# VectorE's second operand kept in PSUM: taps in a bank of their own, gates, residuals and rotations written back

## The reference

```
u = x*(1+sc1) + sh1                     # sc, sh, g from silu(c) @ w_ada
z = u @ w_in + b_in                     # 78 tiles of 128 columns
A: mLSTM       h = num / max(|den|, exp(-m));  y_a = sigmoid(o) * norm(h)
B: attention with a latent cache (prompt: causal; samples: 1024 past rows in 8 pages)
C: convolution y[t] = b + sum_k w[k]*full[t+k], k = 0..30; silu(norm(y))
D: retention   with q, k rotated: x1*cos - x2*sin, x1*sin + x2*cos
out = (sum_n sigmoid(gates_n) * (y_n @ w_branch_n)) @ w_out
x = norm(ALPHA*x + g1*out)
x = norm(ALPHA*x + g2*ffn(x))           # SwiGLU
```

## Time and profile before

| | us |
|---|---|
| three runs | 1928.85, 1932.64, 1932.87; median 1932.64 |
| profiled execution | 1932.92 |
| its span, first to last instruction | 1931.2 |
| PE, weight loads, DVE, ACT, POOL busy | 1733.7, 1490.1, 933.2, 740.0, 694.8 |
| mean granted PE clock | 0.941 of the upper level |

### The profile page before, as it was taken

The page is one execution under the profiler, slowest core; times in us unless marked ns, Lnnn a source line. Parts: engine busy times, 40 slices in busy tenths (PEclk is TensorE's granted clock), DMA queues, the critical chain, the costliest instruction groups (busy, mean ns, idle before and its releaser), DMA issues. The chain is left out here.

```text
span 1931.2 us, 30401 instructions
## 1 busy us (share of the span) xinstructions
PE 1733.7 (90%) x10994; PEld 1490.1 (77%) x10994; DVE 933.2 (48%) x1937; ACT 740.0 (38%) x1122; POOL 694.8 (36%) x418
## 2 busy tenths in 40 slices
PE   3899899998799979999839998999987999799997
PEld 1788789886377759999718987888853788599996
DVE  1454577468631563333323535774785315633333
ACT  1456434333334244443224564342233341544422
POOL 0434546545023313332113445455540233133321
PEclk8899999999899989999969999999997999899999
DMA  9242365246754354444072432652666643544440
GB/s 357 88 177 93 98 105 183 102 154 229 304 205 165 133 199 155 150 152 153 23 282 88 183 110 76 106 195 88 205 234 254 240 169 109 207 146 150 153 151 30
DMA packets 81184, 309.12 MB, mean 160 GB/s; under 512 B 23746, under 2 KB 33282, under 8 KB 50946
## 3 DMA queue, kind: packets, MB, share of 16 engines
q1 hardware_dynamic: 81026, 307.09, 46.3%
HBM read 291.81 MB, written 15.25 MB: 159 GB/s over the span
## 5 line engine op out<-in xcount | busy, mean ns | idle before, releaser
L1980 POOL TENSOR_TENSOR wlx<-ring,wh 128x1024 fp32r<-128x1024 f32 x172 | 410.7, 2388 | 754.8 <-ACT wh L1030 749.9
L430 PE MATMUL zps<-uhi,wh 128*128 128x320 f32 x1232 | 387.3, 326 | 0.0
L431 PE MATMUL zps<-ulo,wh 128*128 128x320 f32 x1232 | 374.1, 315 | 0.0
L1030 ACT ACTIVATE wh<-ring 128x1024 fp32r<-128x1024 f32 x172 | 182.3, 1060 | 394.8 <-PE zps L431 262.8
L2072 POOL TENSOR_TENSOR wlo<-ring,whi 128x1024 fp32r<-128x1024 f32 x66 | 161.9, 2452 | 367.2 <-ACT whi L1030 367.2
L430 PEld LDWEIGHTS zps<-uhi,wh 128*128 128x128 f32 x1232 | 240.3, 195 | 12.8 <-issue 8.4
L431 PEld LDWEIGHTS zps<-ulo,wh 128*128 128x128 f32 x1232 | 240.6, 195 | 0.8
L889 PE MATMUL zps<-xhi,whi 128*128 128x320 f32 x704 | 220.1, 313 | 2.3 <-DVE xlo L1942 2.0
L891 PE MATMUL zps<-xhi,wlo 128*128 128x320 f32 x704 | 219.1, 311 | 0.0
L890 PE MATMUL zps<-xlo,whi 128*128 128x320 f32 x704 | 219.1, 311 | 0.0
L435 PE MATMUL zps<-uhi,wlx 128*128 128x320 f32 x1248 | 211.4, 312 | 0.0
(11 more groups left out here) (268 smaller groups left out, 2573.6 us busy)
## 6 DMA issues: line engine op xcount, KB each, us to landing
ring<-wpack_dram SPq DMA_DIRECT2D x222, 1024.0 KB, 4.9
arena<-cache_dram SPq DMA_DIRECT2D x128, 320.0 KB, 4.6
arena<-stateA_dram SPq DMA_DIRECT2D x2, 2064.0 KB, 9.8
o_cn_s<-arena SPq DMA_DIRECT2D x2, 2064.0 KB, 11.1
arena<-stateD_dram SPq DMA_DIRECT2D x2, 2048.0 KB, 11.8
o_ret_s<-arena SPq DMA_DIRECT2D x2, 2048.0 KB, 11.5
x<-o_y SPq DMA_DIRECT2D x2, 1280.0 KB, 7.5
o_y<-x SPq DMA_DIRECT2D x4, 640.0 KB, 3.0
```

The source lines that it names most:

```text
L430: nc.tensor.matmul(o, hi[:, k * P:(k + 1) * P], xh[:, k, :], start=k == 0, stop=False)
L431: last = nc.tensor.matmul(o, hi[:, k * P:(k + 1) * P], xl[:, k, :], start=False, stop=False)
L1030: return nc.scalar.activation(out, in_, func, **kw).then_inc(*ev(sem, label))
L1980: G().tensor_tensor(wlx[:, n % RING, half], ring[:, n % RING, half], wh[:, i, :], ALU.subtract).then_inc(*ev("pool_l", (q, i)))
```

## The change

Four `mps` banks are left to PE, and the fifth, `taps_ps`, is DVE's alone for the taps: two tiles of 256 columns fill it. The partial sums stay there; the last tap of a tile writes to `y`, and the tiles 2 and 3 wait for the last tap of 0 and 1. In `rotate` the sin halves come first and the cos product is written over the tile's own `zps` bank, which is then released by the sum. In `gated` the product of the first branch goes straight to `gsum`, with no copy; the others write the product over the bank and add it from there. In the residual the gated product is written over the bank, which is released by the sum (`"r"`) in place of the product (`"g"`). The denominators read `num` from PSUM twice, as max(-den, floor) and then max(den, that), with two instructions where there were three (copy, absolute value, maximum). What is computed stays the same.

```diff
--- before.py
+++ after.py
@@ -340,7 +340,8 @@
         cnp = vm[:].rearrange("p h t -> p (h t)")[:, 0:H * W].rearrange("p (h d) -> p h d", h=H)
 
         zps = [ctx.enter_context(nc.psum_tensor(f"zps{i}", [P, 512], F32)) for i in range(3)]
-        mps = [ctx.enter_context(nc.psum_tensor(f"mps{i}", [P, 512], F32)) for i in range(5)]
+        mps = [ctx.enter_context(nc.psum_tensor(f"mps{i}", [P, 512], F32)) for i in range(4)]
+        taps_ps = ctx.enter_context(nc.psum_tensor("taps_ps", [P, 512], F32))
         banks = {}
 
         FIRST_FFN = BLOCKS.index(("ffn", 0))
@@ -385,7 +386,7 @@
                 @block.tensor
                 def _(pe):
                     zi, mi, bi, turned = [0], [0], [0], [0]
-                    zfree, mfree = [None] * 3, [None] * 5
+                    zfree, mfree = [None] * 3, [None] * 4
 
                     def bank(kind, name, freed_by):
 
@@ -678,7 +679,7 @@
                     conv_tiles(3, lambda: row_scores(2), lambda: outputs("a", 0, W))
 
                     def turned_tile(x_, j, *fill):
-                        in_tiles((f"{x_}{j}", f"{x_}{j + 1}"), [("dve_dk", ("t3", x_, h)) for h in (j, j + 1)], fill=fill)
+                        in_tiles((f"{x_}{j}", f"{x_}{j + 1}"), [("dve_dk", (x_, h)) for h in (j, j + 1)], fill=fill)
 
                     def plain_tile(x_, j, *fill):
                         in_tiles((f"{x_}{j}", f"{x_}{j + 1}"), [("act_d", (x_, h)) for h in (j, j + 1)], fill=fill)
@@ -869,7 +870,7 @@
                         q = SPLIT.index(("out", i))
                         for j in range(2):
                             d = 2 * i + j
-                            split_tile(q, n, j, ("wo", d), ("dve_r", ("g", 1, d)), ghi, glo, ("act_go", "dve_gl") if d == 0 else None)
+                            split_tile(q, n, j, ("wo", d), ("dve_r", ("r", 1, d)), ghi, glo, ("act_go", "dve_gl") if d == 0 else None)
                             if d >= 2:
                                 mean_part(1, d - 2)
                         block_end[n] = ("pe_z", ("wo", 2 * i + 1))
@@ -904,7 +905,7 @@
                             last.then_inc(*ev("pe_z", name))
                     pe.wait_ge(*at("dve_f", FT - 1))
                     for d in range(KC):
-                        ps = bank("z", ("fo", d), ("dve_r", ("g", 2, d)))
+                        ps = bank("z", ("fo", d), ("dve_r", ("r", 2, d)))
                         for j in range(FT):
                             i = d * FT + j
                             if i % 16 == 0:
@@ -1643,11 +1644,10 @@
                             out = hh[0:tn, t, 2 * hp:2 * hp + 2, :]
                             if X == "a":
                                 den, rec = stats[0:tn, 80:82], stats[0:tn, 82:84]
-                                V().tensor_copy(rec, num[:, :, P]).then_inc(*ev(s, ("dc", t, hp)))
-                                dve.wait_ge(*at(s, ("dc", t, hp)))
-                                V().scalar_tensor_tensor(out=den, in0=rec, scalar=-1.0, in1=rec, op0=ALU.mult, op1=ALU.max).then_inc(*ev(s, ("abs", t, hp)))
-                                dve.wait_ge(*at(s, ("abs", t, hp)))
-                                V().tensor_tensor(den, den, col4[0:tn, t, 64 + 2 * hp:66 + 2 * hp], ALU.max).then_inc(*ev(s, ("den", t, hp)))
+                                floor = col4[0:tn, t, 64 + 2 * hp:66 + 2 * hp]
+                                V().scalar_tensor_tensor(out=rec, in0=num[:, :, P], scalar=-1.0, in1=floor, op0=ALU.mult, op1=ALU.max).then_inc(*ev(s, ("neg", t, hp)))
+                                dve.wait_ge(*at(s, ("neg", t, hp)))
+                                V().tensor_tensor(den, num[:, :, P], rec, ALU.max).then_inc(*ev(s, ("den", t, hp)))
                                 dve.wait_ge(*at(s, ("den", t, hp)))
                                 V().reciprocal(rec, den).then_inc(*ev(s, ("rec", t, hp)))
                                 dve.wait_ge(*at(s, ("rec", t, hp)))
@@ -1720,12 +1720,12 @@
                         if h == 0:
                             dve.wait_ge(*at("pe_m", ("a", "st", 3)))
                         ps, bias = z(f"{x_}{h}"), sw(f"{x_}{h}")
-                        V().scalar_tensor_tensor(out=dst, in0=ps[:, 0:T], scalar=bias, in1=cs("cosD"), op0=ALU.add, op1=ALU.mult).then_inc(*ev("dve_dk", ("t1", x_, h)))
                         for i, (to, of) in enumerate((((0, 64), (64, 128)), ((64, 128), (0, 64)))):
                             V().scalar_tensor_tensor(out=std[to[0]:to[1], :], in0=ps[of[0]:of[1], 0:T], scalar=bias[of[0]:of[1]], in1=cs("sinD")[of[0]:of[1]],
-                                                   op0=ALU.add, op1=ALU.mult).then_inc(*ev("dve_dk", (f"t{2 + i}", x_, h)))
+                                                   op0=ALU.add, op1=ALU.mult).then_inc(*ev("dve_dk", (f"t{1 + i}", x_, h)))
+                        V().scalar_tensor_tensor(out=ps[:, 0:T], in0=ps[:, 0:T], scalar=bias, in1=cs("cosD"), op0=ALU.add, op1=ALU.mult).then_inc(*ev("dve_dk", ("t3", x_, h)))
                         dve.wait_ge(*at("dve_dk", ("t3", x_, h)))
-                        V().tensor_tensor(dst, dst, std[:], ALU.add).then_inc(*ev("dve_dk", (x_, h)))
+                        V().tensor_tensor(dst, ps[:, 0:T], std[:], ALU.add).then_inc(*ev("dve_dk", (x_, h)))
 
 
                     dve.wait_ge(C.sem("in_hist"), 16)
@@ -1737,13 +1737,16 @@
                         for i in range(first, last):
                             j, k = 2 * (i // (2 * CW)) + i % 2, i % (2 * CW) // 2
                             wk = smallw[:, SM["cw"] + j * CW + k:SM["cw"] + j * CW + k + 1]
-                            o, src = y[:, 2, j, 0:SEQ], ucp[:, j, k:k + SEQ]
+                            part_sum, src = taps_ps[:, j % 2 * SEQ:(j % 2 + 1) * SEQ], ucp[:, j, k:k + SEQ]
+                            o = part_sum if k < CW - 1 else y[:, 2, j, 0:SEQ]
                             if k == 0:
                                 dve.wait_ge(*at("dve_c", ("glu1", j)))
+                                if j >= 2:
+                                    dve.wait_ge(*at("dve_c", ("tap", j - 2, CW - 1)))
                                 nc.vector.tensor_scalar(o, src, wk, sw("cb", j), ALU.mult, ALU.add).then_inc(*ev("dve_c", ("tap", j, k)))
                             else:
                                 dve.wait_ge(*at("dve_c", ("tap", j, k - 1)))
-                                nc.vector.scalar_tensor_tensor(out=o, in0=src, scalar=wk, in1=o, op0=ALU.mult, op1=ALU.add).then_inc(*ev("dve_c", ("tap", j, k)))
+                                nc.vector.scalar_tensor_tensor(out=o, in0=src, scalar=wk, in1=part_sum, op0=ALU.mult, op1=ALU.add).then_inc(*ev("dve_c", ("tap", j, k)))
 
                     rotate("dk", 0)
                     rotate("dk", 1)
@@ -1769,13 +1772,11 @@
                             dve.wait_ge(*at("act_gt", (n, d)))
                             ps = z(("br", n, d))
                             if n == GATE_ORDER[0]:
-                                V().tensor_tensor(gt[:, k, :], ps[:, 0:T], gt[:, k, :], ALU.mult).then_inc(*ev("dve_br", ("first", d)))
-                                dve.wait_ge(*at("dve_br", ("first", d)))
-                                V().tensor_copy(gsum[:, d, :], gt[:, k, :]).then_inc(*ev("dve_br", (n, d)))
+                                V().tensor_tensor(gsum[:, d, :], ps[:, 0:T], gt[:, k, :], ALU.mult).then_inc(*ev("dve_br", (n, d)))
                             else:
-                                V().tensor_tensor(g, ps[:, 0:T], g, ALU.mult).then_inc(*ev("dve_br", ("t", n, d)))
+                                V().tensor_tensor(ps[:, 0:T], ps[:, 0:T], g, ALU.mult).then_inc(*ev("dve_br", ("t", n, d)))
                                 dve.wait_ge(*at("dve_br", ("t", n, d)))
-                                V().tensor_tensor(gsum[:, d, :], gsum[:, d, :], g, ALU.add).then_inc(*ev("dve_br", (n, d)))
+                                V().tensor_tensor(gsum[:, d, :], ps[:, 0:T], gsum[:, d, :], ALU.add).then_inc(*ev("dve_br", (n, d)))
 
                     for t in range(3):
                         tokens("d", t)
@@ -1899,12 +1900,12 @@
                                         split(q)
                             ps = z((name, d))
                             dve.wait_ge(*at("dve_mod", 11 if which == 1 else 23))
-                            nc.vector.tensor_scalar_mul(tmp[:, d % 2, 0:SEQ], ps[:, 0:SEQ], mod[:, g + d, 0:1]).then_inc(*ev("dve_r", ("gp", which, d)))
-                            nc.vector.tensor_tensor(tmp[:, d % 2, SAMP].rearrange("p (b t) -> p b t", b=NB), ps[:, SAMP].rearrange("p (b t) -> p b t", b=NB),
+                            nc.vector.tensor_scalar_mul(ps[:, 0:SEQ], ps[:, 0:SEQ], mod[:, g + d, 0:1]).then_inc(*ev("dve_r", ("gp", which, d)))
+                            nc.vector.tensor_tensor(ps[:, SAMP].rearrange("p (b t) -> p b t", b=NB), ps[:, SAMP].rearrange("p (b t) -> p b t", b=NB),
```

(2 more changed lines are left out.)

## The result

The changed kernel takes **1916.3 us** (median of 11 runs) beside 1932.64 for the kernel before; the ratio is 0.9917, 95% interval 0.9901 to 0.9932. One of the 11 took 3379.28 us, for a reason that nothing here shows, and is left out of the ratio; the other ten lie between 1910.85 and 1923.88. That is 16.3 us less, by the ratio 16.0. Forecast were 1921.5 and 11.3 less, with 1913 to 1938 as the range. The profiled execution took 1919.91 us around a span of 1918.3.

The account below looks back on a forecast made before the run. PE, busy 90% of the span, was taken to bound the kernel. A layer gains 5.45+1.1+2.9-0.5-3.3 = 5.65 us, two layers 11.3; 1932.9-11.3 = 1921.6, given as 1921.5, with 8 in 10 from 1913 to 1938.

Parts of the forecast that it names:

- Denominators: Ahead of the scores behind `weigh`: PE starts 3.25 us sooner and the clock stays up, 2.2; 5.45 us a layer gained.
- Rival A: Behind the denominators the clock stays low, as 2 us of idle remain; without 2.2 us a layer, 1926; chance 0.20.
- Rotations: DVE's rotation sums lose their stalls, but PE's waits name none of them: 0 gained.
- Taps: DVE's five batches of taps, pitch 0.42 us with the sum in PSUM: 4.0 us a layer gained, 0.5 lost.
- rivals B and E: B: PSUM writes slow the taps, 1951 at pitch 0.67, chance 0.14. E: scalars in SBUF still stall, 1939, chance 0.02.
- First batch: Taps end some 9 us sooner, so the token copies no longer hold the first scores: 1.1 us a layer gained.
- Second batch: Taps behind which no PE wait ends: 0 gained.
- Fourth batch: 26 taps take 10.9 us in place of 17.2, so PE's L757 no longer waits: 2.9 us a layer gained.
- Third batch: PE's L757 waits for the copy behind these taps, so each slower tap is PE's loss: 0.5 us a layer.
- Four banks: PE's matmuls wait for bank releases in heads (1.75), last state group (0.9), three more places (0.65): 3.3 us a layer lost.
- Rival C: Four banks cost more than their sum: twice it, 1928, or 1937 if the clock also falls; chance 0.14.
- Rival D: The gain ends on a weight block's transfer, bound by the queue; the denominators' 5.45 would go: 1932; chance 0.10.

Follow-up runs that it names:

- e_den: The kernel before with only the denominators' two instructions, five matmul banks; 1911.78 us, ratio 0.9908.
- e_after: The changed kernel measured and profiled again, the same program; 1915.25 us, ratio 0.9914 to the kernel before.
- e_taps: The kernel before with four matmul banks and the taps accumulated in the fifth; 1930.57 us, ratio 1.0007.
- e_four: The kernel before with four matmul banks in place of five, the fifth unused; 1947.68 us, ratio 1.0088.
- e_rot: The kernel before with only the rotations summed from PSUM, five matmul banks; 1923.41 us, ratio 0.9968.
- e_notaps: The changed kernel with the taps back in SBUF and five matmul banks; 1907.35 us, ratio 0.9881 to the kernel before.

## Why the prediction came out right, and which steps did not

*Total.* The mechanism was right: an operand in PSUM ends the stalls, and only where PE waits for DVE does it pay. -11.3 was forecast and -16.3 measured. But four terms were far too small, three gains (10.9 forecast and 18.7 measured, 0 and 7.1, 7.0 and 17.1) and one loss (6.6 and 17.2), and what they missed cancelled in large part. That the sum came out within 5 us is luck as much as reckoning.

- *Denominators, 5.45 a layer forecast, 9.35 measured alone.* The place itself agrees: -6.0 in e_den against 3.25 for the idle plus 2.2 for the clock, plus 0.8 since five banks let the scores wait only 1.20. (The "idle of 5.5" counts the gate row's product as over after 0.5 us; the row has 4.97.) In the whole change it gave 2.3 and 3.6 in the two layers, 3.8 and 3.6 in e_after: the gate row waits 1.92 and the clock falls after all. Rival A was true there in half. The failed step is the one behind the denominators, what stands late next: I priced the wait of L641 for L1696 only as something that four banks would lengthen by 0.9. It went instead, 5.5 a layer in e_den, since DVE's last scaling escaped a GpSimd operation. In the whole change two waits of 0.9 and 0.5 are left there, and it gave 2.0 and 3.7 in one profile, 1.2 twice in the other.
- *Rotations, "0. [...] PE's waits name none of them".* Measured alone 3.5 a layer. The wait names L1696, which stands behind head norm and rotations in DVE's order; a line that no wait names was on the path of one that is named. Gates and residuals: 0 forecast, +2.4 measured with an interval that reaches no change.
- *Taps, 3.5 a layer forecast net, 8.6 measured* (e_taps against e_four). The pitch was right: 0.42 taken, 0.395 measured, and rivals B and E are out (no tap over 488 ns). First batch: 1.1 forecast; L1568 is gone from the waits. Second batch: "no PE wait ends on what stands behind it: 0" failed against e_four, where GpSimd, held by the taps, was what PE waited for: 2.7 a layer between the two columns. Fourth batch: 2.9 forecast, 5.2 to 5.8 seen when the values of sample 1 end, since L761's sixteen matmuls take 1.95 us at the upper clock. That the load of the next pages "moves with them" was right: PE waits for them 5.35 us before, 5.73 and 5.34 after; where some 4 us were lost again behind them, it was the clock. Third batch: 0.5 forecast as lost, 0.15 seen (L758 waits 1.04 in place of 0.89).
- *Four banks, 3.3 a layer forecast, 8.6 measured* (e_four). The places of the sum were wrong in part: the last state group lost 0.7 in waits (L642, 3.52 in place of 2.79) where 0.9 was forecast, and the heads 1.15 in waits where it was 1.75. Not in the sum stood the clock behind the gate row (1.9 there with the wait) and branch 3 (2.9 in the second layer, 2.3 in the first, GpSimd's wait above). The samples' 1.4 is within the spread of one profile. "From above, twice the sum" was too low, since the lower level behind the gate row lasted 10 us in place of 6.7. Rival C, taken alone, was true; it was paid for by the terms above.
- *Rival D is out.* PE's waits for weight blocks are 54.9 us in 14 before, 57.3 in 14 in the changed kernel and 55.3 in e_after: they did not grow by what the others lost.

What stays open. Alone, the parts add by their ratios to -19.9 us, the whole is -16.0 and -16.6 in two measurements; the intervals (about 6 us on the sum of four) don't tell these apart, so whether the parts disturb each other isn't shown. e_den's and e_rot's second-row gain is one and the same wait. e_notaps, with both, is clearly faster than e_rot, but not told apart from e_den (0.9881, 0.9855 to 0.9907, beside 0.9908, 0.9891 to 0.9925). Why one handover takes 0.46 and another 0.28 us for the same two instructions isn't shown either: it goes with the number of instructions ahead of it, and at retention's head norm it is 0.28 in every kernel. What decides whether the taps in SBUF or GpSimd's subtraction stands, and whether the lower level behind a page load lasts 6.8 or 13.7 us, is open, too.

## What to carry to other kernels

Before a DVE change is priced at nothing, walk back along DVE's order from every wait of PE for DVE, not only from the lines that the wait names: what stands ahead of it on the engine is on the path too. Where two engines meet at a fixed pitch (here a 2.4 us GpSimd subtraction every 4.8 us), ask how far each end is from a collision: 0.09 us more of lead was worth 5.5 us a layer, and no sum of durations shows it. Profile the same program twice before reading a stretch: here two profiles of one kernel differed by 9 us. And a PSUM bank given to one user for a whole layer can be lent while that user is idle: 11 to 14 us here for a few lines.

## What the runs showed of the hardware

- DVE writing PSUM costs about 8 ns for 256 columns (480 against 472 ns with the same operands), a chain through one bank none beyond that; reading the second operand from PSUM is no dearer than from SBUF (472 against a median of 476). The Trainium skill, VectorE: DVE Perf Modes, The TRN2 errata, has 120 fixed cycles for a PSUM source against 58; no such difference stands in these rows, and the measurement decides.
- An operation with one tensor was caught too: four scalings of 64x128 (L1674, SBUF to SBUF) take 1.55 us free and 3.61 beside a GpSimd subtraction, ending with it; the fourth alone takes 0.34 and 2.48. The prediction had used only half of the Trainium skill's section (SBUF — State Buffer, Who interferes with whom), which frees an operation with one SBUF input only outside the two-port modes. It also says that a one-source `tensor_scalar` from SBUF to SBUF can enter a mode that takes the port shared with GpSimd. This trace agrees, and that half could have pointed to the head norm.
- GpSimd can be the one that is held: one subtraction of 128x1024 took 10.89 us beside 28 taps with two operands in SBUF (e_four), in place of 2.4 to 2.6, and ended 2.2 us behind the last of them. Beside taps with the sum in PSUM none took over 3.3.
- Idle times of PE of 1.20, 1.97 and 4.97 us behind the same work were followed by no fall, 3.4 and 6.8 us at the lower clock level. The length of the idle alone does not decide it: in e_notaps the same 1.20 was followed by a fall of 3.4 us, and behind the wait for cache pages one program had 13.7 us at the lower level after 5.73 us of idle, and 6.8 after 5.34.
